# Turning the second layer's input with VectorE squares and SBUF transfers in place of TensorE transposes

## The chip, the cores and the metric

The kernel runs on one core of a Trainium2 chip. The time is the device time of one execution in microseconds; a time stated for a kernel is the median of several runs. One profiled execution gives the trace from which all durations here are read.

## The reference

Two layers (`DEPTH = 2`) of a decoder trunk over 256 tokens of width 2048, all in float32:

```python
def _layer(x, mem, positions, w_in, ...):
    (r_q, ..., z) = _split_cols(x @ w_in, IN_SPLITS)
    # four head groups: retention, latent attention, mLSTM, memory attention
    # (the last one also needs mem @ w_mem_kv)
    y = jnp.concatenate([ret, mla, mls, memo], axis=-1) * jax.nn.silu(z)
    y = y @ w_out
    return _layernorm(DEEPNORM_ALPHA * x + y, ln_g, ln_b)
```

The output of the first layer is the input `x` of the second. It is produced with tokens on the partitions, and the second layer's product `x @ w_in` wants it with features on the partitions, so it has to be turned.

## The kernel before, in words

**The stream.** Every large product is a stream of 304 slots for each layer (`SLOTS`), one slot for a tile of 128 rows of weights. Slots 0 to 15 are `memv` and 16 to 31 are `memk` (the memory's values and keys: they need `mem` alone, not `x`); slot 32 is the first of `lx0`, the first product that needs the layer's input. Float32 is multiplied as two float32r parts, high and low: ScalarE copies a weight tile to `hi` (L1067), VectorE subtracts to get `lo` (L1418), TensorE does `hi` with both parts of the input (L1331, L1332; L1346 in the layout "feat") and `lo` with the high part (L1335; L1352). `raw` has room for four pairs of slots (`RAW = 4`), `hi` and `lo` for five slots (`RING = 5`), so ScalarE and VectorE run at most five slots ahead of TensorE. SyncE (SP) loads `raw` by pairs: pair m holds slots 2m and 2m+1, and its load is issued only when `lo` of slot 2m-7 is done (L678).

**The order.** All other work is hung into this stream by tables that are written out by hand: `LATER_ACT`, `LATER_DVE` and `LATER_PE` say for the second layer after which slot of its own queue an engine does which step. Each engine, and SP too, works strictly in its own order, so a step that waits holds all that is behind it in its queue.

**The turn before.** After the first layer's normalisation ScalarE writes the normalised X in eight blocks of 128x512 (`normalise`, L845, from slot 8 to slot 18), each with its own count on `normed`. TensorE turns it in eight steps `xT` (L1115), two after each of slots 18, 22, 26 and 30, four 128x128 transposes in each, into a PSUM bank. ScalarE takes the high part from there with the gain and offset of the norm applied (`x_hi`, L863, after slots 23, 24, 27, 28, 31, 32, 35 and 36), VectorE the low part (`x_lo`, L1470 and L1477: two 128x256 scale-and-add operations to `tmp`, one subtraction). TensorE waits at slots 32, 34, 36 and 38 for `x_lo` 1, 3, 5 and 7 (L1324).

**The kernel's other turns** are made in another way: VectorE turns 32x32 squares within a block, the squares go out to DRAM (`TURN_OUT_AT`, L741) and come back in four transfers of 32 partitions each (`TURN_IN_AT`, L755, tile `turn`), which put each square in its place.

The buffer Y holds the first layer's input, later the gated product of the first layer, and from pair 22 of the second layer on its small weights (`wukv`, `wuq`, L714 and L716).

Of the kernel before, what the change touches and what calls it, by code (L numbers as in the profile page):

```python
# [130 lines left out]
def _put(table, slot, *step):  # L131
    table.setdefault(slot, []).append(step)


for _j in range(8):
    _put(LATER_PE, 18 + _j // 2 * 4, "xT", _j)
for _h in range(HEADS):
    _put(PE_AT, (71, 75, 81, 87)[_h], "mem_scores", _h)
    _put(PE_AT, 156, "mla_scores", _h)
# [14 lines left out]

ACT_AT = {}
for _j in range(8):
    _put(LATER_ACT, 8 + 3 * _j // 2, "normalise", _j)
    _put(LATER_ACT, 23 + _j // 2 * 4 + _j % 2, "x_hi", _j)
    _put(FIRST_ACT, 15 + 2 * _j, "x_hi", _j)
    if _j:  # L160
        _put(FIRST_ACT, 2 * _j - 1, "m_hi", _j + 1)
# [24 lines left out]


DVE_AT = {}
for _j in range(8):
    _put(LATER_DVE, (24, 26, 28, 30, 32, 34, 37, 38)[_j], "x_lo", _j)  # L190
    _put(FIRST_DVE, 16 + 2 * _j, "x_lo", _j)
    _put(FIRST_DVE, 22 + 2 * _j, "angles", _j)
    if _j > 2:
        _put(FIRST_DVE, 2 * _j - 1, "m_lo", _j + 1)
    _put(DVE_AT, (49, 50, 51, 52, 55, 57, 59, 60)[_j], "conv", _j)
    _put(LATER_DVE, 248 + _j, "gain", _j)
    _put(LATER_DVE, 256 + 2 * _j, "offset", _j)
# [8 lines left out]
for _s, *_step in [  # L206
# [109 lines left out]
def build_trunk(nc, a, out):  # L316
    ctx = ExitStack()
    with ctx:
# [3 lines left out]
        def signal(name, per_layer, before=0, step=1):  # L322
            return Signal(ctx.enter_context(nc.semaphore(name)), per_layer, before, step)
# [23 lines left out]
        def both(i, size):  # L347
            with nc.sbuf_tensor(f"B{i}r", [P, 4 * SEQ], F32R) as same_place:
                pass
            return sb(f"B{i}", [P, size]), same_place  # L350

        row_of = {i: both(i, 4 * SEQ) for i in (1, 2, 4, 5, 6, 7, 8, 9)}
        row_of[0] = both(0, NT * HEADS * (HD + 1))
        cols, stats = sb("cols", [P, NCOLS]), sb("stats", [P, 8, 6])
        row_of[3] = both(3, 4 * (SEQ + PAD))
# [22 lines left out]


        gb0 = gb0_place[:, :].rearrange("p (a n) -> p a n", a=2)  # L380
        xT0 = Y[:, :].rearrange("p (j w) -> p j w", j=8)
        memT = [B[i][:, 0:4 * SEQ] for i in range(4)]
        turn1 = B[4][:, 0:NT * (FR + FM)].rearrange("p (i f) -> p i f", i=NT)
# [70 lines left out]


        early = [Br[i][:, :].rearrange("p (a k t) -> p a k t", a=2, k=2) for i in (1, 2, 3, 0)]

        def y_part(part, j):

# [75 lines left out]
        first_rows = signal("first_rows", 0)  # L535
        finished, gained, diag_done = signal("finished", 0), signal("gained", 0), signal("diag_done", 0)
        scaled, copied = signal("scaled", 0), signal("copied", 0)
        first_gain = signal("first_gain", 0)
        stored = signal("stored", 0, step=16)
        dve_own, act_own = signal("dve_own", 0), signal("act_own", 0)  # L540

# [132 lines left out]
        def _(sp):  # L674
            for l in range(DEPTH):
                for m in range(PAIRS):
# [30 lines left out]
                          .then_inc(lw_in.sem, 16)  # L707
                    if m == 22:

                        if l == 0:  # L710
                            sp.wait_ge(x_lo.sem, x_lo.at(0, 7))
                        else:
                            sp.wait_ge(y_lo.sem, y_lo.at(l - 1, 7))
                        sp.dma_start(Y[:, 0:1024], a["wukv"][l:l + 1, :].rearrange("o (p n) -> p (o n)", p=P))\  # L714
                          .then_inc(mlaw_in.sem, 16)
                        sp.dma_start(Y[:, 1024:3328], a["wuq"][l:l + 1, :].rearrange("o (p n) -> p (o n)", p=P))\  # L716
                          .then_inc(mlaw_in.sem, 16)
# [15 lines left out]
                    if m == 57:  # L733
                        sp.wait_ge(mrow_out.sem, mrow_out.at(l, 0))
                        wait_job(sp, l, ("ml_q", 1))
                        sp.dma_start(B[3][:, 0:1024], a["mrow"].rearrange("h t -> (h t)").partition_broadcast(P))\
                          .then_inc(mrow_in.sem, 16)
                    if m in TURN_OUT_AT:
                        name = TURN_OUT_AT[m]
                        sp.wait_ge(squared[name].sem, squared[name].at(l, squared[name].per_layer - 1))  # L740
                        sp.dma_start(a["turn"][TURNS.index(name), :, 0:TURN_COLS[name]], squares[name]).then_inc(turn_out[name].sem, 16)  # L741
# [75 lines left out]
        def _(act):  # L817
# [20 lines left out]
            for l in range(DEPTH):  # L838
# [15 lines left out]
                def x_hi_(j):  # L854
                    if l == 0:
                        act.wait_ge(xT_in[j // 2].sem, 16)
                        act.activation(xh[:, 2 * j:2 * j + 2, :], xT0[:, j, :].rearrange("p (k t) -> p k t", k=2),
                                       ACT.Copy).then_inc(x_hi.sem, 1)
                        return
                    wait_job(act, l, ("xT", j))  # L860
                    act.wait_ge(cols_in.sem, cols_in.at(l, 0))
                    for k in (2 * j, 2 * j + 1):
                        m = act.activation(xh[:, k, :], bank(l, ("xT", j))[:, (k % 2) * 256:(k % 2 + 1) * 256], ACT.Identity,  # L863
                                           scale=cols[:, C_LNG + k:C_LNG + k + 1], bias=cols[:, C_LNB + k:C_LNB + k + 1])
                    m.then_inc(x_hi.sem, 1)

# [221 lines left out]
        def _(pe):  # L1088
# [5 lines left out]
            for l in range(DEPTH):  # L1094
                def take(*job):

                    b, u = bank_of(l, job)
                    stand_alone(pe)
                    pe.wait_ge(bank_read[b].sem, bank_read[b].at(0, u - 1))
                    return work[:, b, :]  # L1100

                def turn(dst, src):
                    return pe.transpose(dst, src, ident[0:src.shape[0], 0:src.shape[0]])  # L1103
# [8 lines left out]
                def both(parts, at):  # L1112
                    return tuple(at(x) for x in parts)

                def xT(j):  # L1115
                    pe.wait_ge(ident_in.sem, 16)
                    pe.wait_ge(normed.sem, 2 * (j // 2) + 2)
                    o = take("xT", j)
                    for kk in range(2):
                        for i in range(NT):  # L1120
                            m = turn(o[:, kk * 256 + i * P:kk * 256 + (i + 1) * P],
                                     X[:, i, (2 * j + kk) * P:(2 * j + kk + 1) * P])
                    m.then_inc(job_done.sem, 1)

                def mem_scores(h):
                    if h == 0:
                        pe.wait_ge(kq_split.sem, kq_split.at(l, 3))
# [135 lines left out]
                def ret_out(q):  # L1263
# [3 lines left out]
                    for h in (2 * q, 2 * q + 1):  # L1267
# [3 lines left out]
                        m = pe.matmul(o[:, c + P:c + 256], pt[:, 2 * P:3 * P], rv[:, 1, v], start=False, stop=True)  # L1271
                    m.then_inc(job_done.sem, 1)

                steps = {"xT": xT, "mem_scores": mem_scores, "mem_out": mem_out,
                         "ml_fold": ml_fold, "ml_q": ml_q, "gateT": gateT,
                         "ml_scores": ml_scores, "ml_out": ml_out, "mla_qr": mla_qr, "mla_kn": mla_kn,
                         "mla_qn": mla_qn, "mla_v": mla_v,
# [114 lines left out]
        def _(dve):  # L1392
# [47 lines left out]
            for l in range(DEPTH):  # L1440
# [23 lines left out]
                def x_lo_(j):  # L1464
                    dve.wait_ge(x_hi.sem, x_hi.at(l, j))
                    src, part = xT0[:, j, :].rearrange("p (k t) -> p k t", k=2), xh[:, 2 * j:2 * j + 2, :].bitcast(F32)
                    if l:
                        dve.wait_ge(cols_in.sem, cols_in.at(l, 0))
                        for k in (2 * j, 2 * j + 1):
                            m = dve.tensor_scalar(tmp[:, (k % 2) * 256:(k % 2 + 1) * 256],  # L1470
                                                  bank(l, ("xT", j))[:, (k % 2) * 256:(k % 2 + 1) * 256],
                                                  cols[:, C_LNG + k:C_LNG + k + 1], cols[:, C_LNB + k:C_LNB + k + 1],
                                                  ALU.mult, ALU.add)
                        m.then_inc(free_bank(l, "xT", j), 1)
                        wait_read(dve, l, ("xT", j))
                        src = tmp[:, :].rearrange("p (k t) -> p k t", k=2)
                    dve.tensor_tensor(xl[:, 2 * j:2 * j + 2, :], src, part, ALU.subtract).then_inc(x_lo.sem, 1)  # L1477
                    if l:
                        dve.wait_ge(x_lo.sem, x_lo.at(l, j))

                def gain(b):
                    cb, i = divmod(b, 2)
                    blk = X[:, i, cb * 512:(cb + 1) * 512]
                    if b == 0:
                        dve.wait_ge(gb0_in.sem, 16)
                        wait_job(dve, l, ("xT", 7))
                    link(dve.tensor_tensor(blk, blk, gb0[:, 0, cb * 512:(cb + 1) * 512], ALU.mult))

                def offset(b):
# [384 lines left out]
                def residual(c, *only):  # L1874
# [8 lines left out]
                    for i in only or range(NT):  # L1883
# [4 lines left out]
                steps = {"angles": angles_, "lo": lo_of, "x_lo": x_lo_, "m_lo": m_lo, "gain": gain, "offset": offset, "kept_lo": kept_lo_, "y_lo": y_lo_, "memv": memv, "mem_max": mem_max, "mem_norm": mem_norm,  # L1888
                         "mem_out": out_pair("mem_out", memo), "conv": conv, "rms": rms_, "ckv": ckv, "cqn": cqn_,
                         "kpe_rope": kpe_rope, "gates": gates, "gate_scan": gate_scan, "skip": skip, "ones": ones,  # L1890
                         "turn": turn, "turn_head": turn_head, "turn_rotary": turn_rotary, "cT": cT_, "gate_squares": gate_squares_, "ml_gap": ml_gap, "ml_weigh": ml_weigh, "ml_out": ml_out,
# [158 lines left out]
```

## Time and profile before

| | |
|---|---|
| time, median of 3 runs | 892.41 us (891.58 to 893.32) |
| time of the profiled execution | 892.57 us |
| its span | 890.8 us |
| granted TensorE clock | 0.999 |
| PE busy | 883.6 us, 99% of the span |
| VectorE busy | 661.1 us, 74% |
| ScalarE busy | 487.2 us, 55% |

The span runs from the first to the last instruction of the profile; some 1.8 us of the execution's time lie around it. "Busy" is the time in which an engine had an instruction in work. The second layer's stream begins at about 440.6 us of the span.

### The profile page before, as it was taken

How to read it: one execution, taken by the hardware profiler on the slowest of the kernel's cores; microseconds unless marked ns; L12 is line 12 of the kernel's file. 1: busy time of each engine (PE TensorE's matmuls, PEld its weight loads, DVE VectorE, ACT ScalarE, POOL GpSimd, SP SyncE). 2: the span in 40 equal slices, each digit the busy share in tenths (PEclk: the TensorE clock that was granted, in tenths of full speed). 3: DMA queues.
4: the chain of work that ended last, by engine and by line, in shares of the span. 5: the costliest groups of instructions: out<-in, count | busy, mean ns of one | idle time of the engine just before them, and what ended most of it. 6: DMA issues, size and time to landing. Idle time of an engine off the chain costs nothing.

```text
span 890.8 us, 13199 instructions
## 1 busy us (share of the span) xinstructions
PE 883.6 (99%) x4540; PEld 758.6 (85%) x4540; DVE 661.1 (74%) x1314; ACT 487.2 (55%) x914; POOL 17.4 (2%) x18
## 2 busy tenths in 40 slices
PE   9999999999999999999999999999999999999997
PEld 7888998888888888888888889888888888887896
DVE  6869697878595677766668887868677748679865
ACT  6655785545455346544476556746355553564541
POOL 0000000000000000000000000000000001000001
PEclk9999999999999999999999999999999999999999
DMA  9796587547679687665675966885484875976932
GB/s 357 281 337 200 147 268 254 177 135 229 209 219 320 210 261 247 201 190 189 191 200 185 306 229 180 258 260 169 140 280 143 292 217 165 258 220 224 356 103 95
DMA packets 70802, 198.21 MB, mean 223 GB/s; under 512 B 9288, under 2 KB 22864, under 8 KB 70096
## 3 DMA queue, kind: packets, MB, share of 16 engines
q1 hardware_dynamic: 70160, 196.33, 68.2%
q10 hardware_dynamic: 576, 1.05, 0.4%
q8 instruction: 36, 0.59, 0.3%
q14 instruction: 30, 0.25, 0.1%
HBM read 182.38 MB, written 14.95 MB: 222 GB/s over the span
## 4 chain that ended last, share of the span: by engine, by line
PE 97%; issue 1%; DVE 1%; DMA 0%; ACT 0%; POOL 0%; POOLq 0%; ACTq 0%; DVEq 0%
PE acc L1331 24%; PE acc L1332 24%; PE acc L1335 24%; PE acc L1346 10%; PE acc L1352 5%; PE work L1110 1%; PE work L1109 1%; PE work L1108 1%; PE work L1237 1%; PE work L1236 1%; PE work L1103 0%; DMA B<-in_mem_t 0%; PE work L1259 0%; PE work L1248 0%; PE work L1176 0%
## 5 line engine op out<-in xcount | busy, mean ns | idle before, releaser
L1418 DVE TENSOR_TENSOR lo<-raw,hi 128x512 fp32r<-128x512 f32 (+2 forms) x607 | 387.4, 656 | 181.4 <-ACT hi L1067 167.6
L1067 ACT ACTIVATE hi<-raw 128x512 fp32r<-128x512 f32 (+2 forms) x607 | 355.4, 603 | 297.5 <-PE acc L1335 229.2
L1331 PE MATMUL acc<-hi,xx 128*128 128x512 f32 (+2 forms) x768 | 285.4, 374 | 0.9 <-DVE xx L1514 0.9
L1332 PE MATMUL acc<-hi,xx 128*128 128x512 f32 (+2 forms) x768 | 283.5, 372 | 0.0
L1335 PE MATMUL acc<-lo,xx 128*128 128x512 f32 (+2 forms) x768 | 223.0, 372 | 0.0
L1331 PEld LDWEIGHTS acc<-hi,xx 128*128 128x128 f32 x768 | 144.6, 188 | 24.9 <-DVE xx L1514 1.3
L1332 PEld LDWEIGHTS acc<-hi,xx 128*128 128x128 f32 x768 | 144.6, 188 | 23.5
L1335 PEld LDWEIGHTS acc<-lo,xx 128*128 128x128 f32 x768 | 140.4, 188 | 24.6
L1346 PE MATMUL acc<-xx,hi 128*128 128x512 f32 x384 | 96.1, 392 | 0.0
L1346 PEld LDWEIGHTS acc<-xx,hi 128*128 128x128 f32 x384 | 69.3, 189 | 12.6
L1352 PEld LDWEIGHTS acc<-xx,lo 128*128 128x128 f32 x384 | 52.4, 190 | 3.7
L1352 PE MATMUL acc<-xx,lo 128*128 128x256 f32 x384 | 53.5, 282 | 0.0
L1331 PE MATMUL acc<-hi,mm 128*128 128x512 f32 x126 | 49.5, 392 | 0.0
L1332 PE MATMUL acc<-hi,mm 128*128 128x512 f32 x126 | 49.1, 389 | 0.0
L1335 PE MATMUL acc<-lo,mm 128*128 128x512 f32 x126 | 38.8, 389 | 0.0
L1335 PEld LDWEIGHTS acc<-lo,mm 128*128 128x128 f32 x126 | 23.7, 188 | 5.0
L1331 PEld LDWEIGHTS acc<-hi,mm 128*128 128x128 f32 x126 | 23.7, 188 | 4.9 <-issue 0.2
L1332 PEld LDWEIGHTS acc<-hi,mm 128*128 128x128 f32 x126 | 23.7, 188 | 4.7
L793 POOL TENSOR_TENSOR rstd<-stats,half 128x4 f32<-128x4 f32 (+1 forms) x6 | 9.6, 1594 | 351.0 <-DVE stats L1838 221.6
L970 ACT ACTIVATE B<-work 128x512 f32<-128x512 f32 x12 | 7.2, 596 | 14.7 <-PE work L1110 14.7
L1822 DVE TENSOR_TENSOR probT<-work,const 128x384 f32<-128x384 f32 x8 | 4.4, 554 | 13.4 <-PE work L1260 13.4
L935 ACT ACTIVATE prob<-prob,nmax 128x128 f32<-128x128 f32 (+1 forms) x16 | 7.2, 448 | 10.4 <-DVE nmax L1808 10.4
(346 smaller groups left out, 975.0 us busy)
## 6 DMA issues: line engine op xcount, KB each, us to landing
raw<-in_w SPq DMA_DIRECT2D x263, 512.0 KB, 4.4
B<-turn SPq DMA_DIRECT2D x80, 128.0 KB, 5.0
raw<-in_w SPq DMA_DIRECT2D x26, 256.0 KB, 2.7
turn<-B SPq DMA_DIRECT2D x12, 512.0 KB, 5.8
raw<-in_w SPq DMA_DIRECT2D x16, 328.0 KB, 3.3
turn<-Y SPq DMA_DIRECT2D x8, 512.0 KB, 5.5
Y<-in_wuq SPq DMA_DIRECT2D x2, 1152.0 KB, 8.8
Y<-in_x_t SPq DMA_DIRECT2D x4, 512.0 KB, 8.7
```

What stands on the lines that cost most here:

```text
L793: return pool.tensor_tensor(dst, src, half[:, 0:n], ALU.pow)
L1067: act.activation(place(l, t, hi), raw[:, s, (t % 2) * w:(t % 2 + 1) * w], ACT.Copy)\
L1108: pe.matmul(o, ah, bh, start=start, stop=False)
L1109: pe.matmul(o, al, bh, start=False, stop=False)
L1110: return pe.matmul(o, ah, bl, start=False, stop=stop)
L1236: pe.matmul(o[:, c0:c1], qnT[:, h, q], knT[:, h, 0:c1 - c0], start=True, stop=False)
L1331: pe.matmul(o, ah[:, q], hi[:, s, 0:w], start=k == 0, stop=False, skip_group_check=name == "memv")
L1332: pe.matmul(o, al[:, q], hi[:, s, 0:w], start=False, stop=False, skip_group_check=name == "memv")
L1335: m = pe.matmul(acc[:, p, i, 0:w], ah[:, i * P:(i + 1) * P], lo[:, s, 0:w], start=False, stop=k == KT - 1, skip_group_check=name == "memv")
L1346: pe.matmul(acc[:, p, j, :], hi[:, (l * SLOTS + t + u) % RING, q], x, start=k + u == 0 and kk == 0, stop=False, skip_group_check=True)
L1352: m = pe.matmul(acc[:, p, j, 0:SEQ], lo[:, s, q], both_parts[:, 2 * k + kk, 0, :], start=False, stop=2 * k + kk == KT - 1, skip_group_chec ...
L1418: dve.tensor_tensor(place(l, t, lo), raw[:, s, (t % 2) * w:(t % 2 + 1) * w], place(l, t, hi).bitcast(F32), ALU.subtract).then_inc(lo_done. ...
```

## The change

TensorE's step `xT` is gone. In its place:

- VectorE does four steps `square_x` after slots 10, 12, 13 and 15: in each, two operations that turn the 32x32 squares of a normalised 128x512 block of X. They write to `x_squares`, 16 KB a partition, in the place of the buffers B4 to B7.
- SP issues sixteen transfers from SBUF to SBUF, four after the weight load of each of the pairs 11, 12, 13 and 14. One moves 32 partitions by four runs of 1 KB, 128 KB in all, from `x_squares` to Y. Ahead of the first SP waits for all four `square_x`.
- ScalarE's `normalise` is at slots 8 to 13. Its `x_hi` are at slots 22 to 29, one a slot, and wait for all sixteen transfers; they read Y in SBUF, in runs of 32 elements, and not a PSUM bank.
- VectorE's `x_lo` are at slots 23, 25, 27, 28, 30, 32, 33 and 35 and read Y.
- `gain` no longer waits for TensorE's last `xT`.

```diff
-for _j in range(8):
-    _put(LATER_PE, 18 + _j // 2 * 4, "xT", _j)
...
-    _put(LATER_ACT, 8 + 3 * _j // 2, "normalise", _j)
-    _put(LATER_ACT, 23 + _j // 2 * 4 + _j % 2, "x_hi", _j)
+    _put(LATER_ACT, 8 + 3 * _j // 4, "normalise", _j)
+    _put(LATER_ACT, 22 + _j, "x_hi", _j)
...
+for _cb in range(4):
+    _put(LATER_DVE, (10, 12, 13, 15)[_cb], "square_x", _cb)
 for _j in range(8):
-    _put(LATER_DVE, (24, 26, 28, 30, 32, 34, 37, 38)[_j], "x_lo", _j)
+    _put(LATER_DVE, (23, 25, 27, 28, 30, 32, 33, 35)[_j], "x_lo", _j)
...
+X_IN_AT = (11, 12, 13, 14)
...
+                    if l and m in X_IN_AT:
+                        if m == X_IN_AT[0]:
+                            sp.wait_ge(x_squared.sem, 4)
+                            sp.wait_ge(y_lo.sem, y_lo.at(l - 1, 7))
+                        q = m - X_IN_AT[0]
+                        for b in range(4):
+                            sp.dma_start(Y[b * 32:(b + 1) * 32, :].rearrange("c (j a n) -> c j a n", j=4, a=4)[:, :, q],
+                                         x_squares[q * 32:(q + 1) * 32, :, b * 256:(b + 1) * 256]).then_inc(xT_in[0].sem, 16)
...
-                    wait_job(act, l, ("xT", j))
+                    act.wait_ge(xT_in[0].sem, 16 + 16 * 16)
...
+                        m = act.activation(xh[:, k, :].rearrange("p (i a r) -> p i a r", i=NT, a=4), x_block(j, k % 2), ACT.Identity,
...
+                def square_x(cb):
+                    dve.wait_ge(normed.sem, 2 * cb + 2)
+                    to = x_squares[:, cb, :].rearrange("p (b i j r) -> p i j b r", b=4, i=NT, j=4)
+                    for i in range(NT):
+                        m = dve.transpose(to[:, i], X[:, i, cb * 512:(cb + 1) * 512].rearrange("p (j b c) -> p j b c", j=4, b=4))
+                    m.then_inc(x_squared.sem, 1)
```

## Rows read from the trace of the kernel before

**Rows 1.** The page: busy time by engine, and the chain that ended last.

```profile
PE 883.6 (99%) x4540; PEld 758.6 (85%) x4540; DVE 661.1 (74%) x1314; ACT 487.2 (55%) x914; POOL 17.4 (2%) x18
PE 97%; issue 1%; DVE 1%; DMA 0%; ACT 0%; POOL 0%; POOLq 0%; ACTq 0%; DVEq 0%
```

**Rows 2.** Timeline, TensorE, slots 16 to 33 (start us, us, engine line op).

```profile
463.06 0.62 PE L1335 MATMUL acc<-lo,mm 128*128 128x512 f32 x2
...
465.78 0.62 PE L1335 MATMUL acc<-lo,mm 128*128 128x512 f32 x2
...
468.03 0.61 PE L1335 MATMUL acc<-lo,mm 128*128 128x512 f32 x2
...
487.53 2.00 PE L1346 MATMUL acc<-xx,hi 128*128 128x512 f32 x8
489.37 1.12 PE L1352 MATMUL acc<-xx,lo 128*128 128x256 f32 x8
490.32 2.00 PE L1346 MATMUL acc<-xx,hi 128*128 128x512 f32 x8
```

**Rows 3.** Chain in order of time, 464 to 490 us: start us, us, what.

```profile
466.40 0.87 PE work L1103 x8
...
485.44 0.88 PE work L1103 x8
```

**Rows 4.** Timeline, ScalarE: slot 8, first `normalise`, slot 22.

```profile
446.09 0.63 ACT L1067 ACTIVATE hi<-raw 128x512 fp32r<-128x512 f32 x1 [0.79 <-PE acc L1335]
446.63 0.80 ACT L845 ACTIVATE X<-X,ln_shift,ln_rstd 128x512 f32<-128x512 f32 x1
...
465.13 0.63 ACT L1067 ACTIVATE hi<-raw 128x512 fp32r<-128x512 f32 x1 [0.79 <-PE acc L1335]
```

**Rows 5.** Timeline, VectorE: `lo` of slot 15, and the first `x_lo`.

```profile
456.22 0.69 DVE L1418 TENSOR_TENSOR lo<-raw,hi 128x512 fp32r<-128x512 f32 x1 [0.61 <-ACT hi L1067]
...
470.02 0.99 DVE L1470 TENSOR_SCALAR tmp<-work,cols 128x256 f32<-128x256 f32 x2
...
471.77 1.30 DVE L1418 TENSOR_TENSOR lo<-raw,hi 128x512 fp32r<-128x512 f32 x2
```

**Rows 6.** VectorE, groups by form (count, busy us, mean ns of one, idle before).

```profile
L1470 DVE TENSOR_SCALAR tmp<-work,cols 128x256 f32<-128x256 f32 x16 | 7.9, 537 | 0.0
...
L1635 DVE STREAM_TRANSPOSE B<-B 128x1024 f32<-128x1024 f32 x4 | 5.0, 1239 | 0.0
...
L1759 DVE TENSOR_SCALAR B<-B,mv,rstd 128x128 f32<-128x128 f32 x16 | 4.4, 342 | 0.0
...
L1582 DVE TENSOR_SCALAR B<-B,cols 128x256 f32<-128x256 f32 x8 | 2.8, 350 | 0.1
```

**Rows 7.** Timeline, ScalarE: a pair that reads turned blocks in SBUF.

```profile
340.16 0.89 ACT L877 ACTIVATE B3r<-B,cols 128x256 fp32r<-128x256 f32 x2
```

**Rows 8.** Timeline, SP's queue: the load of `wuq`, the four transfers of one turn.

```profile
492.27 0.43 SPq L716 DMA_DIRECT2D Y<-in_wuq  x1
...
503.45 1.75 SPq L755 DMA_DIRECT2D B<-turn  x4
```

**Rows 9.** Transfers of the page: count, KB each, median us from issue to landing.

```profile
raw<-in_w SPq DMA_DIRECT2D x263, 512.0 KB, 4.4
B<-turn SPq DMA_DIRECT2D x80, 128.0 KB, 5.0
...
Y<-in_wuq SPq DMA_DIRECT2D x2, 1152.0 KB, 8.8
...
gcol<-tmp SPq DMA_DIRECT2D x8, 2.0 KB, 2.2
```

**Rows 10.** Windows of 1 us: length, granted clock, DMA share, GB/s.

```profile
503.00:504.00 1.00, 1.00 1.01 414
...
507.00:508.00 1.00, 1.00 1.09 222
```

**Rows 11.** The same in a later turn, issued from 665.98 us on.

```profile
669.00:670.00 1.00, 1.00 0.76 173
```

More of the change, by code:

```diff
@@ L350, in both, with both_x @@
             return sb(f"B{i}", [P, size]), same_place
-        row_of = {i: both(i, 4 * SEQ) for i in (1, 2, 4, 5, 6, 7, 8, 9)}
+        turned_place = {}
+        def both_x(i, size):
+            if i == 4:
+                with nc.sbuf_tensor("x_squares", [P, 4, 4 * SEQ], F32) as x_place:
+                    turned_place["x"] = x_place
+            return both(i, size)
+        row_of = {i: both_x(i, 4 * SEQ) for i in (1, 2, 4, 5, 6, 7, 8, 9)}
         row_of[0] = both(0, NT * HEADS * (HD + 1))
@@ L380, in build_trunk @@
         gb0 = gb0_place[:, :].rearrange("p (a n) -> p a n", a=2)
+        x_squares = turned_place["x"]
         xT0 = Y[:, :].rearrange("p (j w) -> p j w", j=8)
@@ L456, in build_trunk, with x_block @@
         early = [Br[i][:, :].rearrange("p (a k t) -> p a k t", a=2, k=2) for i in (1, 2, 3, 0)]
+        def x_block(j, n):
+            return Y[:, j // 2 * 1024:(j // 2 + 1) * 1024]\
+                .rearrange("p (a i j r) -> p j i a r", a=4, i=NT, j=4)[:, j % 2 * 2 + n]
         def y_part(part, j):
@@ L537, in build_trunk @@
         scaled, copied = signal("scaled", 0), signal("copied", 0)
-        first_gain = signal("first_gain", 0)
+        first_gain, x_squared = signal("first_gain", 0), signal("x_squared", 0)
         stored = signal("stored", 0, step=16)
@@ L708, in _ @@
                     if m == 22:
[L710 to L713, printed above, removed]
+                        sp.wait_ge(x_lo.sem, x_lo.at(l, 7))
                         sp.dma_start(Y[:, 0:1024], a["wukv"][l:l + 1, :].rearrange("o (p n) -> p (o n)", p=P))\
@@ L859, in x_hi_ @@
                         return
-                    wait_job(act, l, ("xT", j))
+                    act.wait_ge(xT_in[0].sem, 16 + 16 * 16)
                     act.wait_ge(cols_in.sem, cols_in.at(l, 0))
                     for k in (2 * j, 2 * j + 1):
-                        m = act.activation(xh[:, k, :], bank(l, ("xT", j))[:, (k % 2) * 256:(k % 2 + 1) * 256], ACT.Identity,
+                        m = act.activation(xh[:, k, :].rearrange("p (i a r) -> p i a r", i=NT, a=4), x_block(j, k % 2), ACT.Identity,
                                            scale=cols[:, C_LNG + k:C_LNG + k + 1], bias=cols[:, C_LNB + k:C_LNB + k + 1])
@@ L1113, in both @@
                     return tuple(at(x) for x in parts)
[L1115 to L1123, printed above, removed]
                 def mem_scores(h):
@@ L1272, in ret_out @@
                     m.then_inc(job_done.sem, 1)
-                steps = {"xT": xT, "mem_scores": mem_scores, "mem_out": mem_out,
+                steps = {"mem_scores": mem_scores, "mem_out": mem_out,
                          "ml_fold": ml_fold, "ml_q": ml_q, "gateT": gateT,
@@ L1469, in x_lo_ @@
                         for k in (2 * j, 2 * j + 1):
-                            m = dve.tensor_scalar(tmp[:, (k % 2) * 256:(k % 2 + 1) * 256],
-                                                  bank(l, ("xT", j))[:, (k % 2) * 256:(k % 2 + 1) * 256],
+                            m = dve.tensor_scalar(tmp[:, (k % 2) * 256:(k % 2 + 1) * 256].rearrange("p (i a r) -> p i a r", i=NT, a=4),
+                                                  x_block(j, k % 2),
                                                   cols[:, C_LNG + k:C_LNG + k + 1], cols[:, C_LNB + k:C_LNB + k + 1],
                                                   ALU.mult, ALU.add)
-                        m.then_inc(free_bank(l, "xT", j), 1)
-                        wait_read(dve, l, ("xT", j))
+                        link(m)
                         src = tmp[:, :].rearrange("p (k t) -> p k t", k=2)
@@ L1485, in gain @@
                         dve.wait_ge(gb0_in.sem, 16)
-                        wait_job(dve, l, ("xT", 7))
                     link(dve.tensor_tensor(blk, blk, gb0[:, 0, cb * 512:(cb + 1) * 512], ALU.mult))
@@ L1886, in residual @@
                     return m
-                steps = {"angles": angles_, "lo": lo_of, "x_lo": x_lo_, "m_lo": m_lo, "gain": gain, "offset": offset, "kept_lo": kept_lo_, "y_lo": y_lo_, "memv": memv, "mem_max": mem_max, "mem_norm": mem_norm,
+                steps = {"angles": angles_, "lo": lo_of, "x_lo": x_lo_, "m_lo": m_lo, "square_x": square_x, "gain": gain, "offset": offset, "kept_lo": kept_lo_, "y_lo": y_lo_, "memv": memv, "mem_max": mem_max, "mem_norm": mem_norm,
                          "mem_out": out_pair("mem_out", memo), "conv": conv, "rms": rms_, "ckv": ckv, "cqn": cqn_,
```

## The prediction

> **What bounds the kernel now.** I read the page first. It shows TensorE busy for 99% of the span and holding 97% of the chain that ended last [rows 1], so the reader is to see that a microsecond off TensorE's queue is a microsecond off the time, and that every wait put on it costs in full. Next the chain in order of time around the turn: the transposes are on it, in four pieces of eight [rows 3]. Then each engine's timeline, to see how far ScalarE and VectorE run ahead, and last SP's queue, the landing times and the DMA windows, since the change moves the turn there.
>
> **A clock of slots.** Two slots of the memory products take 465.78 - 463.06 = 2.72 us on TensorE, 1.36 each; the slot with transposes behind it takes 468.03 - 465.78 = 2.25 [rows 2]. Without any transpose slot 19 would begin 0.45 us after 465.78, at 466.23, and so slot 23 at 466.23 + 4 x 1.36 = 471.67. The pair of slots 32 and 33 begins at 487.53 and a pair takes 2.79 us [rows 2]; without the four groups it would begin near 484.0, and the pair 36 and 37 at 489.6.
>
> **Removed.** Four pieces of 0.87 or 0.88 us [rows 3]: 3.5 us off TensorE, all on the path. This is the whole gain; nothing else on TensorE changes.
>
> **Added ahead of the transfers.** ScalarE now does eight `normalise` in slots 8 to 13. From 446.09, with 0.54 us for a `hi` and 0.80 for a block [rows 4], that ends at 446.1 + 6 x 0.54 + 8 x 0.80 = 455.7. TensorE does not reach slot 13 until 458, so this is hidden by the lead of four to five slots. The squares are not shown at 128x512; 1024 columns take 1.24 us [rows 6], so one lies between 0.62 (half) and 0.69 (a 128x512 subtraction [rows 5]). I take 0.65, eight of them 5.2 us. They hold up `lo` of slots 11 to 15: `lo` 10 is done near 450.7, then five `lo` at 0.61 and the squares: 450.7 + 3.1 + 5.2 = 459.0, against 456.9 before [rows 5]. TensorE wants `lo` 16 at 463, so this too costs nothing. But the transfers begin only then: SP passes its wait at about 459.5.
>
> **The transfers.** SP needs 1.75 us for four issues [rows 8], so 7.0 for sixteen and some 1.2 for the three weight loads between them: the last is issued at 467.7 at the earliest. Landing time is the unknown. From below: the only SBUF-to-SBUF transfers of the trace, of 2 KB, land after 2.2 us [rows 9], which gives 469.9; with the 5.0 us of the 128 KB transfers of a turn [rows 9] it is 472.7. By bytes: sixteen times 128 KB is 2.1 MB, and the weight loads of pairs 11 to 14 are another 2.1 MB in the same engines. The weight loads move at 414 GB/s when the engines are full [rows 10], 1.27 us each, 5.1 in all. The turns' transfers, of the same shape (32 partitions, runs of 1 KB) but from DRAM, pull the rate down to 222 and 173 GB/s [rows 10, 11], in windows in which weights still take a part. I take 200 GB/s for them: 10.5 us. Sum 15.6 from 459.5: 475.1, and with the first transfer's latency T = 475.5 for the landing of the last. With 173 GB/s and a microsecond more it is 477.7. The range of T is 469.9 to 477.7.
>
> The Trainium skill says in "SBUF — State Buffer", section "Door 1: The DMA port swizzle", that a transfer on 32 partitions reaches only half of SBUF's ports, measured there at 189 GB/s for 1 MiB. The rows agree as far as they go (173 and 222 GB/s where the turns run); by its figure 2.1 MB would take an estimated 11.1 us in place of 10.5, and the sum would rise by 0.6.
>
> **Who waits.** `x_hi` 0 stands behind slot 22 in ScalarE's queue and waits for all sixteen. ScalarE starts `hi` 22 at 465.13 [rows 4], so it is there by 465.8 and stands until T; behind it in its queue is `hi` 23, for which VectorE's `lo` 23 and TensorE's slot 23 wait. An `x_hi` pair from SBUF costs 0.8 [rows 7], then `hi` 0.63: `hi` 23 is there at T + 1.4. TensorE wants it at 471.67. By this alone TensorE loses T - 470.2: at 475.5, 5.3 us. Before, the same step hung behind a transpose of slot 18, and ScalarE never stood.
>
> VectorE stands as well, and has all eight `x_lo` left. One took 1.75 us (470.02 to 471.77 [rows 5]). Reading SBUF, its two scale-and-add operations cost between 0.35 each (one column operand [rows 6]) and 0.54 as before; with two column operands 128 columns already take 0.34 [rows 6], so I take 0.41, and 1.5 for an `x_lo` (1.4 to 1.75). From T + 1.4 to the end of `lo` 37 it has fifteen `lo` at 0.61, eight `x_lo` and the `memk` turn of 1.24: 9.2 + 12.0 + 1.24 = 22.5, so T + 23.9. TensorE wants `lo` 37 at 489.6 + 2.3 = 491.9 (the `lo` part of a pair starts 1.84 into it, 487.53 to 489.37 [rows 2], its second half 0.5 later). Loss: T - 468.0; with the bounds of `x_lo`, T - 468.9 to T - 466.1. This is the larger one and decides: at 475.5 it is 7.5 us. After slot 38 VectorE's `lo` alone is less than TensorE's slot, and the lead comes back; `raw` is not late, for the pairs up to 14 have long been loaded.
>
> **Sum.** -3.5 + 7.5 = +4.0 us on the profiled execution's 892.57 us (span 890.8, 1.8 around it), 896.6; that execution lies 0.16 above the median, so I say 896.5. Bounds: T 469.9 with the cheapest `x_lo` gives -3.5 + 1.0 = -2.5, 890.1; T 477.7 with the dearest gives -3.5 + 11.6 = +8.1, 900.7. The gain is eaten from T = 471.5 on.
>
> **Rivals.**
>
> *The transfers are quick and the gain stays.* The place is ScalarE's wait at slot 22. If a transfer within SBUF has no DRAM in its way, only SP's issue holds it, and T is 469.9: with the cheapest `x_lo` 890.1, and if ScalarE's and VectorE's lead covers all of it, 892.57 - 3.5 = 889.1. It decides below T = 471.5, and shows by over 0.2% below 469.7. For it speak the 2.2 us of the small ones; against it SP's last issue at 467.7 and the rates of the turns. The Trainium skill ("DMA: Bandwidth & Descriptors", section "Why small descriptors are slow (HBM only)") says that transfers within SBUF do not pay for small descriptors; by its 435 GB/s for the fabric the bytes would need an estimated 4.8 us, and no run here shows it. Chance 0.10.
>
> *A draw.* The transfers move nearly like weights: T between 469.7 and 473.3, landing 5 us after the last issue. The loss on TensorE then equals the gain within 1.8 us: at T = 472.7 it is 4.7 - 3.5 = +1.2, 893.8, and about 892.5 in the middle. The change does what it says, and the time does not move. Chance 0.20.
>
> *The lateness is passed on.* SP issues the second layer's `wuq` at pair 22, when `lo` 37 is done; it takes 8.8 us to land [rows 9], and ScalarE needs it at slot 45. Before, TensorE reached slot 46 (seven pairs of 2.79 after 487.53 [rows 2], 507.1) 15 us after the issue at 492.3 [rows 8]; after, with `lo` 37 only just in time, about 11. With 8.8 + 0.83 + 0.63 for the first of its steps 0.5 us is left, and a transfer that is 2 us slower costs 1.5. With the high bounds: 898.5 to 901. Chance 0.15.
>
> **How the numbers follow.** Forecast as above (T 473.3 to 477.7, loss 5.3 to 9.7 us, 894.4 to 898.8): 0.55; quick 0.10; draw 0.20; passed on 0.15. A measurement of this kernel tells some 0.2%, 1.8 us, from no change. Faster by more than that: the quick case, 0.10. Within it: the draw, 0.20. Slower: 0.70. The range leaves out the quick end below 891.0 and the far end of the last case above 900.7: some 0.09 and 0.06, and the rest is in the width of T.
>
> **What the profile after would show.** No L1103 on TensorE between slots 18 and 30 and slots of 1.36 us up to slot 22 (the 3.5 us). A wait of ScalarE on the DMA of Y of some 9 to 10 us behind `hi` 22 (T at 475.5); under 5 us would be the quick case. TensorE idle 4 to 6 us at slot 23, with ScalarE's `hi` as the releaser, then small waits on `lo` up to slot 37, 7 to 8 us together. DMA windows near 200 to 270 GB/s at full share between 460 and 475. Squares of 0.62 to 0.69 us; `x_lo` of 1.4 to 1.6. What would make me wrong above all: a rate of the SBUF transfers over 300 GB/s, or a start of the transfers well ahead of 459.5.

## The result, and the profile after

| | before | after |
|---|---|---|
| time, median | 891.78 us (891.58 to 893.32) | 901.57 us (900.13 to 901.90) |
| profiled execution | 892.57 us | 900.13 us |
| its span | 890.8 us | 898.3 us |
| granted TensorE clock | 0.999 | 0.996 |
| PE busy | 883.6 us | 882.1 us |

The kernel became slower by 1.04%: the ratio is 1.0104, 95% interval 1.0093 to 1.0114. Both columns have five runs of one session, and the rows below come from the profiled executions. These differ by 7.5 us and the medians by 9.8; after's profiled execution is the shortest of its five (1.4 us under their median), before's lies 0.8 above its own.

The page of after, its first busy row and the shares of the chain, against [rows 1]:

```profile
PE 882.1 (98%) x4508; PEld 756.4 (84%) x4508; DVE 662.6 (74%) x1322; ACT 486.6 (54%) x914; POOL 17.8 (2%) x18
PE 91%; DVE 2%; DMA 2%; issue 2%; ACT 1%; SPq 1%; POOL 0%; POOLq 0%; ACTq 0%; DVEq 0%
```

TensorE has 32 instructions fewer, the transposes, but its share of the chain that ended last fell from 97 to 91%: the end now hangs on other engines for part of the time. The waits of 440 to 520 us say where (engine, line, waited for: us in total, times, longest):

```profile
ACT xx L883 <- DMA Y<-x_squares: 11.7, 1, 11.7
...
PE acc L1341 <- ACT hi L1087: 7.3, 1, 7.3
ACT mm L930 <- DMA Y<-in_wuq: 2.7, 1, 2.7
ACT hi L1087 <- DMA raw<-in_w: 2.2, 2, 1.5
...
PE acc L1362 <- DVE lo L1428: 1.0, 1, 1.0
PE acc L1356 <- ACT hi L1087: 0.9, 1, 0.9
...
PE acc L1345 <- DVE lo L1428: 0.3, 1, 0.3
```

The rows that begin with PE add up to 9.5 us; before, TensorE was busy for every one of these 80 us. The wait of the first row (ScalarE, for the transfers) is the cause of the 7.3 us of TensorE. ScalarE's timeline, against [rows 4]:

```profile
465.16 0.63 ACT L1087 ACTIVATE hi<-raw 128x512 fp32r<-128x512 f32 x1 [0.79 <-PE acc L1345]
477.51 1.09 ACT L883 ACTIVATE xx<-Y,cols 128x256 fp32r<-128x256 f32 x2 [11.72 <-DMA Y<-x_squares]
478.51 0.61 ACT L1087 ACTIVATE hi<-raw 128x512 fp32r<-128x512 f32 x1
479.03 1.08 ACT L883 ACTIVATE xx<-Y,cols 128x256 fp32r<-128x256 f32 x2
```

`hi` of slot 22 (465.16) begins within 0.03 us of where it began before. Then ScalarE stands for 11.72 us in `x_hi` 0, until 477.51, which is T, the landing of the last transfer. `hi` 23 follows it. TensorE's timeline, against [rows 2]; the rows with a bracket are its waits:

```profile
471.25 0.61 PE L1345 MATMUL acc<-lo,mm 128*128 128x512 f32 x2
479.17 0.79 PE L1341 MATMUL acc<-hi,mm 128*128 128x512 f32 x1 [7.31 <-ACT hi L1087]
...
481.90 0.46 PE L1341 MATMUL acc<-hi,mm 128*128 128x512 f32 x1
...
490.12 0.74 PE L1345 MATMUL acc<-lo,mm 128*128 128x512 f32 x2 [0.26 <-DVE lo L1428]
...
493.46 1.98 PE L1356 MATMUL acc<-xx,hi 128*128 128x512 f32 x8
...
502.48 0.71 PE L1362 MATMUL acc<-xx,lo 128*128 128x256 f32 x4 [0.98 <-DVE lo L1428]
503.03 2.00 PE L1356 MATMUL acc<-xx,hi 128*128 128x512 f32 x8
...
515.23 2.08 PE L1356 MATMUL acc<-xx,hi 128*128 128x512 f32 x8 [0.87 <-ACT hi L1087]
```

Read against an even pace of 1.36 us a slot and 2.79 a pair, this is an account of all that was lost: slot 23 begins at 479.17 in place of 471.70 (+7.5); slot 23 takes 481.90 - 479.17 = 2.73 us (+1.4); slots 24 to 31 take 11.56 in place of 10.9 (+0.7); the `lo` products of slot 37 wait for VectorE (503.03 - 493.46 less three pairs, +1.2); slot 46 waits for `hi`, behind `wuq` and a late `raw` (515.23 - 503.03 less four pairs, +1.0). That is 11.8 lost and 3.5 gained, +8.3, of which 7.5 are left at the end of the span.

VectorE and the queue of SP, against [rows 5] and [rows 8]:

```profile
457.89 1.30 DVE L1494 STREAM_TRANSPOSE x_squares<-X 128x512 f32<-128x512 f32 x2
...
479.76 0.73 DVE L1480 TENSOR_SCALAR tmp<-Y,cols 128x256 f32<-128x256 f32 x2
480.53 0.69 DVE L1486 TENSOR_TENSOR xx<-tmp,xx 128x512 fp32r<-128x512 f32 x1
481.26 0.69 DVE L1428 TENSOR_TENSOR lo<-raw,hi 128x512 fp32r<-128x512 f32 x1
```

```profile
459.22 2.55 SPq L756 DMA_DIRECT2D Y<-x_squares  x4
461.81 0.60 SPq L700 DMA_DIRECT2D raw<-in_w  x1
...
469.34 2.54 SPq L756 DMA_DIRECT2D Y<-x_squares  x4
```

Two squares take 1.30 us in the row and the next `lo` begins 1.22 after them; an `x_lo` takes 481.26 - 479.76 = 1.50. The first issue is at 459.22, but four take 2.55 us, not 1.75, and the sixteenth issue, begun at 471.27, ends at 471.9. That transfer lands 6.22 us after its issue began:

```profile
471.27 6.22 DMA Y<-x_squares
...
502.73 0.43 SPq L726
...
503.68 9.49 DMA raw<-in_w
```

These are pieces of the chain in order of time. L726 issues `wukv`; `wuq` follows at 503.21, 10.9 us later than before. The last row is the load of pair 23 (slots 46 and 47), issued directly behind the two. It lands after 9.49 us, at 513.2, and ScalarE, which has waited 2.7 us for `wuq`, waits another 0.71 for it ahead of `hi` of slot 46. So a late `raw` has a part in the 1.0 us lost at slot 46. The windows (length, busy time of the engines, granted clock, DMA share, GB/s), against [rows 10, 11]; rows without the busy times are from a view that leaves them out:

```profile
459.00:463.00 4.00, 4.00 (x19) 3.33 (x18) 2.75 (x5) 1.83 (x3) 0.00 (x0) 1.00 0.80 233
463.00:467.00 4.00, 4.00 (x20) 3.30 (x19) 3.76 (x6) 1.33 (x3) 0.00 (x0) 1.00 1.05 276
467.00:471.00 4.00, 4.00 (x19) 3.32 (x18) 0.80 (x2) 0.00 (x0) 0.00 (x0) 1.00 1.03 243
471.00:475.00 4.00, 0.86 (x4) 0.38 (x2) 0.00 (x0) 0.00 (x0) 0.00 (x0) 1.00 1.08 248
475.00:476.00 1.00, 0.59 0.75 135
476.00:477.00 1.00, 0.50 0.21 67
...
480.00:482.00 2.00, 2.00 (x6) 1.51 (x6) 1.88 (x4) 2.00 (x5) 0.00 (x0) 0.50 0.48 121
482.00:484.00 2.00, 2.00 (x10) 1.65 (x9) 1.81 (x4) 2.00 (x5) 0.00 (x0) 1.00 0.42 162
```

The DMA engines are full from 463 to 475 and move 243 to 276 GB/s in those windows: that is what the transfers and the weights get together. After 476 they are nearly idle, though the last transfer is seen to land only at 477.5. The granted clock falls in the window from 475 to 476 (0.59) and is 0.50 (1.2 GHz) from 476 to 482, after TensorE had stood since 471.9, and 1.00 again from 482 on; hence the slot of 2.73 us.

### The profile page after: what moved, and what is told of

Read it like the earlier page. It is cut to its first block, busy times and chain, and to the rows that moved or that the text cites. A ratio compares the mean times of both kernels' runs of the same rounds, so it can differ in the third digit from the quotient of the medians.

```text
span 898.3 us, 13151 instructions
## 1 busy us (share of the span) xinstructions
PE 882.1 (98%) x4508; PEld 756.4 (84%) x4508; DVE 662.6 (74%) x1322; ACT 486.6 (54%) x914; POOL 17.8 (2%) x18
## 4 chain that ended last, share of the span: by engine, by line
PE 91%; DVE 2%; DMA 2%; issue 2%; ACT 1%; SPq 1%; POOL 0%; POOLq 0%; ACTq 0%; DVEq 0%
PE acc L1342 23%; PE acc L1341 23%; PE acc L1345 23%; PE acc L1356 8%; PE acc L1362 4%; PE work L1130 1%; PE work L1129 1%; PE work L1128 1%; DMA raw<-in_w 1%; DVE lo L1428 1%; DMA Y<-x_squares 1%; PE work L1246 1%; PE work L1247 1%; ACT hi L1087 1%; SPq L756 0%
## 5 line engine op out<-in xcount | busy, mean ns | idle before, releaser
L1345 PEld LDWEIGHTS acc<-lo,mm 128*128 128x128 f32 x126 | 23.9, 190 | 5.6 <-DVE lo L1428 0.7
L883 ACT ACTIVATE xx<-Y,cols 128x256 fp32r<-128x256 f32 x16 | 8.7, 591 | 11.7 <-DMA Y<-x_squares 11.7
L1837 DVE TENSOR_TENSOR probT<-work,const 128x384 f32<-128x384 f32 x8 | 4.4, 554 | 12.6 <-PE work L1270 12.6
```

The costliest lines, as they stand in the source:

```text
L1345: m = pe.matmul(acc[:, p, i, 0:w], ah[:, i * P:(i + 1) * P], lo[:, s, 0:w], start=False, stop=k == KT - 1, skip_group_check=name == "memv")
```

## The experiments

Ten kernels ran, in three groups, each group beside runs of the kernel before on its own chip (medians 891.51, 891.52 and 891.41 us). Unless it is said otherwise, an edit is made to the kernel after, and a ratio is to the kernel before, with its 95% interval.

### The gain alone, and the traffic alone

```diff
-X_IN_AT = (11, 12, 13, 14)
+X_IN_AT = ()
...
-                    act.wait_ge(xT_in[0].sem, 16 + 16 * 16)
```

This leaves out the transfers. `x_hi` and `x_lo` read the normalised X where it lies, so the second layer works on an input that isn't turned; squares and all other steps stay.

> The kernel after without the sixteen transfers; x_hi and x_lo read unturned X in SBUF in the same shape, so the second layer computes with an unturned input. Theory (the gain is the 3.5 us of transposes and all the rest of the result is the wait): 891.8 - 3.5 = 888.3 us, no idle of TensorE at slot 23, granted clock full. Rival (the squares on VectorE or the SBUF reads cost the path something by themselves): 890 us or more.

Measured: 888.70 us (887.90 to 891.52), ratio 0.9970 [0.9960, 0.9979]. So the transposes on TensorE were worth 2.8 us by the medians and 3.4 by the shortest executions (887.90 against before's 891.32), where 3.5 had been put down. TensorE has no wait from 440 to 520 us in this run; squares, the earlier `normalise` and the steps that read SBUF cost little or nothing.

The second kernel issues all sixteen transfers, but still nobody on ScalarE or VectorE waits for them or reads what they bring; the input is again not turned. SP alone waits, before the buffers of the squares and Y are written again:

```diff
                     if m == 20:
+                        if l:
+                            sp.wait_ge(xT_in[0].sem, 16 + 16 * 16)
...
-                    act.wait_ge(xT_in[0].sem, 16 + 16 * 16)
```

> As the run without transfers, but all sixteen transfers are issued as in the kernel after and nobody on ScalarE or VectorE waits for them (SP waits for them before it loads over their source and destination). The input of the second layer is again unturned. Theory (only the wait of ScalarE costs): within 1 us of the run without transfers, 888 to 889.5. Rival (4.2 MB in 16 us hold up the weight loads themselves): ScalarE waits for raw at slots 24 to 30 and the time is 892 or more.

Measured: 891.50 us (889.24 to 893.17), ratio 0.9992 [0.9981, 1.0004], between the two expected results and nearer to the rival. The two intervals do not meet: the traffic by itself takes back 2.8 us, the whole gain, with no wait placed on it. ScalarE's timeline shows how; while the transfers run the load of `raw` is late three times, 2.3 us in all, where there was no such wait before or without the transfers:

```profile
469.14 0.63 ACT L1089 ACTIVATE hi<-raw 128x512 fp32r<-128x512 f32 x1 [0.52 <-DMA raw<-in_w]
...
473.32 0.63 ACT L1089 ACTIVATE hi<-raw 128x512 fp32r<-128x512 f32 x1 [1.05 <-DMA raw<-in_w]
...
477.20 0.63 ACT L1089 ACTIVATE hi<-raw 128x512 fp32r<-128x512 f32 x1 [0.76 <-DMA raw<-in_w]
```

In its windows the DMA engines are at 1.01 to 1.08 of their time from 464 to 476 with 267 to 279 GB/s, against 0.39 to 0.60 before. ScalarE waits for `raw` for 5.9 us in all from 440 to 520 (3.7 without the transfers, all of it after 501 us; none before), and TensorE stands twice:

```profile
493.53 0.71 PE L1364 MATMUL acc<-xx,lo 128*128 128x256 f32 x4 [1.03 <-DVE lo L1430]
...
506.45 1.84 PE L1358 MATMUL acc<-xx,hi 128*128 128x512 f32 x7 [1.06 <-ACT hi L1089]
```

The first is `lo` of slot 37, which without the transfers is in time; the second is slot 46, behind `wuq` and the load of pair 23, for which ScalarE waits 2.1 and 1.46 us here, 1.2 and 1.37 without the transfers.

### Fewer bytes, and a second queue

```diff
-                        for b in range(4):
+                        for b in ((0, 1) if q % 2 == 0 else (2, 3)):
...
-                    act.wait_ge(xT_in[0].sem, 16 + 16 * 16)
+                    act.wait_ge(xT_in[0].sem, 16 + 8 * 16)
```

Eight transfers in place of sixteen; the other half of Y isn't written, and is read as it lies.

> Only eight of the sixteen transfers are sent and waited for (half of Y keeps old values). With 200 GB/s for these bytes the last lands 5.2 us earlier, near 471 to 472, ScalarE's wait is 6 us, TensorE's idle at slot 23 about 1.5 us, the clock does not fall: 893 to 895 us. If a fixed latency and not the amount sets the landing, it stays above 475 and the time above 898.

Measured: 896.86 us (896.53 to 898.25), ratio 1.0057 [1.0042, 1.0072], 2 us above what was expected. T comes 3.7 us earlier, at 473.8: 0.46 us for each 128 KB left out, 283 GB/s at the margin. Eight issues of SP are gone with them, so this run alone doesn't tell bytes from issues; the next one does. The time falls by 4.7. Half of the bytes don't take away half of the 18.3 us from the first issue to T, for weights and latency stay.

```diff
-                        for b in range(4):
+                        for b in range(2):
...
+                    pool.wait_ge(x_squared.sem, 4)
+                    for q in range(4):
+                        for b in (2, 3):
+                            pool.dma_start(Y[b * 32:(b + 1) * 32, :]..., x_squares[...]).then_inc(x_pool.sem, 16)
...
```

The same sixteen transfers, eight of them issued by GpSimd, with ScalarE waiting for both counts.

> Half of each four transfers is issued by GpSimd, which is idle, all eight of them at once when the squares are done, with a count of its own. If SP's issue (0.64 us each, 10.3 us in all) sets the landing, the last transfer lands some 4 to 5 us earlier, near 473, and the time falls to about 896. If the bytes in the DMA engines set it, the landing stays at 476 to 478 and the time at 900 to 902.

Measured: 901.28 us (901.13 to 901.53), ratio 1.0103 [1.0088, 1.0118], the time of the kernel after. Its row of issues:

```profile
459.66 4.52 POOL L822 DMA_DIRECT2D Y<-x_squares x8 [13.75 <-DVE x_squares L1503]
```

All eight are out by 464.2, yet ScalarE's wait is 12.6 us (11.7 after). From issue to landing GpSimd's take 3.5 to 8.8 us. SP's own eight still stand behind weight loads, so its last issue begins at 470.0, only 1.3 us earlier than after, but that transfer lands after 8.49 us in place of 6.22. So SP's dear issues, though they are on the chain of after, don't set T: issued earlier, the transfers lie longer in the engines, and the bytes set it.

### The shape and the order of the transfers

```diff
-                            sp.dma_start(Y[b * 32:(b + 1) * 32, :].rearrange("c (j a n) -> c j a n", j=4, a=4)[:, :, q],
-                                         x_squares[q * 32:(q + 1) * 32, :, b * 256:(b + 1) * 256]).then_inc(xT_in[0].sem, 16)
+                            sp.dma_start(Y[:, q * 1024 + b * 256:q * 1024 + (b + 1) * 256],
+                                         x_squares[:, q, b * 256:(b + 1) * 256]).then_inc(xT_in[0].sem, 16)
```

Sixteen transfers of the same 128 KB in runs of 1 KB, but over all 128 partitions; the squares don't get to their places.

> The sixteen transfers have the same bytes, the same runs of 1 KB and the same places in SP's queue, but each copies 256 columns of all 128 partitions to the same partitions of Y (so Y gets the squares unplaced, and the input is wrong). If the shape of 32 partitions makes the transfers slow, the last lands near 473 (limited by SP's last issue at 471.9), ScalarE's wait falls from 11.7 to 7 or 8 us and the time to about 896 to 897. If the bytes and the runs of 1 KB within SBUF are slow in any shape, the landing stays at 476 to 478 and the time at 900 to 902.

Measured: 898.47 us (897.45 to 899.38), ratio 1.0077 [1.0064, 1.0091], between the two expected results. ScalarE's wait is 9.86 us, so T comes 1.9 us earlier in its queue, and the time is 3.1 us less. Its windows of 459 to 475 are at 0.75 to 0.91 of the engines' time with 257 to 271 GB/s, the same bytes for less of it. The shape has a part in T, at least 1.9 us of it. How much more is not shown: here the engines are no longer full, SP's last issue begins at 471.30 and its transfer lands 4.61 us later, so SP's issues may hold T in this run. Wide transfers from two queues were not tried. The Trainium skill's rule that a transfer on 32 partitions reaches only half of SBUF's ports ("SBUF — State Buffer", section "Door 1: The DMA port swizzle") points the same way; by its 189 GB/s the forecast T would have been an estimated 476.1, still short of 477.5.

```diff
-                        for b in range(4):
+                        for b in (0, 2, 1, 3):
```

> The kernel after with the four transfers of each group in the order of target partitions 0, 64, 32, 96 (from 0, 32, 64, 96), so that neighbours in the queue write different halves of the partitions. If neighbours in the queue hold each other up because they write the same half, the landing is 2 us or more earlier and the time 898 to 899.5. If not, the landing stays at 477 to 478 and the time at 901 to 902.

Measured: 900.70 us (899.47 to 902.22), ratio 1.0098 [1.0083, 1.0114], and a wait of 12.3 us on ScalarE: no difference that can be told. In its trace one issue of SP took 2.35 us and the last began at 473.3, so T says little here; the time decides.

### The clock

```diff
+for _j in range(4):
+    _put(LATER_PE, 22, "fill", _j)
...
+                def fill(j):
+                    o = take("fill", j)
+                    for n in range(7):
+                        m = pe.matmul(o, mm[:, 0, 0, 0:P], mm[:, 0, :, :].rearrange("p a t -> p (a t)"), start=True, stop=True)
...
```

28 products that nobody uses stand behind slot 22, so that TensorE works through the wait.

> 28 products of 128x512 that nobody reads stand on TensorE behind slot 22, 6.3 us of work in the 7.9 us in which it was idle; nothing else changes. If the low clock after the idle stretch costs the two slow slots (2.73 against 1.36 us), the granted clock stays full and the time falls by 1.4 us, to about 900.2. If the low clock is only seen in the idle stretch and costs nothing, the time stays at 901.6.

Measured: 901.02 us (899.92 to 903.66), ratio 1.0106 [1.0089, 1.0123]. TensorE's timeline:

```profile
471.76 6.51 PE L1140 MATMUL work<-mm 128*128 128x512 f32 x28
479.83 0.50 PE L1350 MATMUL acc<-hi,mm 128*128 128x512 f32 x1 [1.56 <-ACT hi L1089]
...
481.34 0.50 PE L1350 MATMUL acc<-hi,mm 128*128 128x512 f32 x1
```

The windows up to 484 show a granted clock of 1.00, and slot 23 takes 481.34 - 479.83 = 1.51 us in place of 2.73. The time is the same. Slot 23 starts 0.66 us later than after (T was later too), and the wait for the last `lo`, at 503.15, is again 0.67 later: nothing of the faster slot is left there. From T on it is VectorE that sets slot 37, and ScalarE's pair of `x_hi` and `hi` takes 1.50 us (478.51 and 480.01) against TensorE's 1.36. The half clock was real, but it was hidden.

### The wait at another place

```diff
-    _put(LATER_ACT, 22 + _j, "x_hi", _j)
+    _put(LATER_ACT, (31, 31, 32, 33, 34, 35, 36, 37)[_j], "x_hi", _j)
...
-    _put(LATER_DVE, (23, 25, 27, 28, 30, 32, 33, 35)[_j], "x_lo", _j)
+    _put(LATER_DVE, (31, 31, 33, 33, 35, 35, 37, 37)[_j], "x_lo", _j)
```

The `memk` turn of VectorE goes to slot 38, out of the way. The computation is whole.

> The same sixteen transfers at the same places, but x_hi stands behind slots 31 to 37 (from 22 to 29), x_lo behind 31 to 37 and the memk turn behind 38. Theory (the wait stands too early in ScalarE's queue): x_hi 0 comes just as the last transfer lands, TensorE does not idle at slot 23, and only VectorE's eight x_lo before slot 38 cost 1 to 3 us: 889.5 to 891.5. Rival (eight x_lo, eight x_hi and fifteen slots cannot be done between 477.5 and slot 38): a loss of 5 us or more there, 894 or more.

Measured: 896.03 us (893.87 to 897.55), ratio 1.0042 [1.0025, 1.0058]: 5.5 us less than after, and still slower than before. The hole at slot 23 is gone, but two other costs come up, in ScalarE's and in TensorE's timeline:

```profile
473.34 1.16 ACT L1089 ACTIVATE hi<-raw 128x512 fp32r<-128x512 f32 x2 [3.14 <-DMA raw<-in_w]
477.25 1.15 ACT L1089 ACTIVATE hi<-raw 128x512 fp32r<-128x512 f32 x2 [2.75 <-DMA raw<-in_w]
480.41 1.16 ACT L1089 ACTIVATE hi<-raw 128x512 fp32r<-128x512 f32 x2 [2.01 <-DMA raw<-in_w]
```

```profile
485.71 2.06 PE L1358 MATMUL acc<-xx,hi 128*128 128x512 f32 x8 [1.22 <-ACT hi L1089]
489.81 2.11 PE L1358 MATMUL acc<-xx,hi 128*128 128x512 f32 x8 [1.10 <-DVE xx L1488]
494.01 2.11 PE L1358 MATMUL acc<-xx,hi 128*128 128x512 f32 x8 [1.14 <-DVE xx L1488]
498.21 2.12 PE L1358 MATMUL acc<-xx,hi 128*128 128x512 f32 x8 [1.14 <-DVE xx L1488]
```

ScalarE and VectorE reach slots 32 to 38 with little lead, since `raw` was late, and have two `x_lo` of 1.5 us in each pair of slots beside its two `lo`: 4.2 us a pair (489.81 to 494.01), where TensorE needs 2.79. Four waits, 4.6 us, are the remaining loss.

### Half by transfers, half by TensorE

TensorE turns the blocks of `x_hi` 0 to 3 as the kernel before did, behind slots 18 and 22; the sixteen transfers carry only the other half, 64 KB each.

```diff
+for _j in range(4):
+    _put(LATER_PE, 18 + _j // 2 * 4, "xT", _j)
...
-    _put(LATER_ACT, 22 + _j, "x_hi", _j)
+    _put(LATER_ACT, (23, 24, 27, 28, 30, 31, 32, 33)[_j], "x_hi", _j)
...
-for _cb in range(4):
+for _cb in (2, 3):
...
-    _put(LATER_DVE, (23, 25, 27, 28, 30, 32, 33, 35)[_j], "x_lo", _j)
+    _put(LATER_DVE, (24, 26, 28, 30, 32, 33, 35, 36)[_j], "x_lo", _j)
```

> TensorE turns the first half of the features (four of its eight steps, 1.75 us), the squares and transfers the second half, with sixteen transfers of 64 KB, and x_hi 4 to 7 wait for them behind slots 30 to 33. The last transfer lands near 475, x_hi 4 is reached near 478, so nobody waits: half the gain, 891.8 - 1.7 = 890.1. If transfers of half the size are no quicker and late again, TensorE idles at slot 31 and the time is above 893.

Measured: 891.00 us (890.22 to 892.47), ratio 0.9993 [0.9984, 1.0001]. Nobody waits for the transfers, each lands after 2.1 to 3.8 us, and this is TensorE's only wait from 440 to 520 us:

```profile
506.62 2.08 PE L1376 MATMUL acc<-xx,hi 128*128 128x512 f32 x8 [0.42 <-ACT hi L1097]
```

It is the fastest kernel here that computes the whole, and it can't be told from the kernel before: half of 3.5 us is 1.75, and the trace shows part of it going to the same two places, `raw` (ScalarE waits 2.3 us) and `wuq` (2.5 us).

To take `wuq` out, its steps were moved two slots back:

```diff
-    _put(ACT_AT, 45 + _k, "wuq", _k)
-    _put(DVE_AT, 46 + _k, "lo", "wuq", _k)
+    _put(ACT_AT, 47 + _k, "wuq", _k)
+    _put(DVE_AT, 48 + _k, "lo", "wuq", _k)
```

> As the version in which TensorE turns half, and the steps that split wuq stand two slots later, so that its late landing no longer holds hi of slot 46. The 0.7 us of idle TensorE behind it should go: 890.3. If VectorE is the one that is late there (its conv steps begin at slot 49), the time stays at 891 or goes up.

Measured: 892.49 us (891.72 to 893.15), ratio 1.0009 [1.0001, 1.0018]. The wait for `wuq` is gone and a wait for `raw` of 3.7 us stands in the same stretch; TensorE waits 0.6 us for a `lo`. It gained nothing, and the issues of SP say why. The load that is late is that of pair 23 again: issued at 494.36, directly behind `wukv` and `wuq`, it lands after 9.5 us, just when `hi` of slot 46 begins (503.86). The same load takes 9.5 to 9.7 us in the kernel after, without the transfers, with them unread and in the half version; in the kernel before, where it was issued 3.9 us behind `wuq`, it takes 6.0. Moving the steps of `wuq` uncovers that wait; it doesn't take it away.

## Why the prediction was right or wrong

The direction and the mechanism were right: 3.5 us are taken off TensorE, one wait of ScalarE at slot 22 holds `hi` 23, `lo` of slot 37 is late after it, and `wuq` behind that. The time was forecast at 896.5 us and measured at 901.57, beyond the upper bound of 900.7; on the profiled execution the forecast change was +4.0 and the measured one +7.5 us. Two steps of the sum failed. T, the landing of the last transfer, was sized too small: 16.0 us from the first issue, measured 18.3. And what comes behind T was put too low: the term T - 468.0 gives 9.5 us with the measured T, where 10.8 were lost up to slot 38, and slot 46, with `wuq` and `raw` late, was put at nothing and cost 1.0. By the steps:

- **"3.5 us off TensorE."** Right in kind; 2.8 by medians, 3.4 by the shortest executions, when nothing is transferred.
- **Squares, "I take 0.65".** Two in 1.22 to 1.30 us: 0.61 to 0.65. The last ended at 459.2, and SP's first issue is at 459.22 (forecast 459.5).
- **"SP needs 1.75 us for four issues."** 2.55, and the three weight loads between them take 2.2 in place of 1.2. The last issue ends at 471.9, not 467.7. It is wrong, but it costs nothing here: with half the issues on another queue T does not come earlier.
- **"With the first transfer's latency T = 475.5."** This is the term that decides, and it was too small: 477.5. From the first issue on 4.2 MB took 18.3 us, where 16 were forecast. The sum had put weights at 414 GB/s and transfers at 200, one after the other, 15.6 us, a mean of 269 GB/s; the windows of 4 us in which both run show 233 to 276. With the 256 GB/s of 463 to 475 the bytes need an estimated 16.4 us, 0.8 more. The rest lies at the ends: the engines are at 0.80 of their time from 459 to 463, and at 0.21 in the microsecond from 476, while the landing is seen at 477.5; the sum had 0.4 us for all latency. The upper bound, 477.7, held it by 0.2 us. The transfers' narrow shape accounts for at least 1.9 us of T (the wide ones), the order for nothing that the time shows, the bytes for 0.46 us a transfer.
- **"An `x_hi` pair from SBUF costs 0.8."** 0.99 (0.59 an operation); with `hi` 1.50 us. `hi` 23 is there at T + 1.6, forecast T + 1.4.
- **"TensorE loses T - 470.2."** 7.3 by the formula with the measured T, 7.3 in the row of the wait, 7.5 by the pace.
- **"I take 0.41, and 1.5 for an `x_lo`."** 406 ns and 1.50 us.
- **"Loss: T - 468.0."** 9.5 with the measured T. By the account the loss up to slot 38 is 10.8. `lo` 37 is there near 502.3, T + 24.8 in place of T + 23.9: the first `lo` begins 0.2 late, and VectorE stands 0.65 us in three waits before it, two of them for ScalarE's `hi`.
- **"`raw` is not late."** This was wrong, and it was left out of every bound. The transfers alone cost 2.8 us, with `raw` late while they run and again at slot 46; with the wait placed later ScalarE waits 12.5 us for `raw` from 440 to 520, one of the two costs there. In the kernel after itself it is hidden up to T, for ScalarE stands anyway while `raw` comes in, but not at slot 46: the 0.71 us are on TensorE's path, and without them an estimated 0.2 of its 0.87 us of waiting would be left.
- **"The lateness is passed on" (chance 0.15).** It came on top of the forecast: `wuq` was issued at 503.21, ScalarE waited 2.7 us for it and 0.7 for the `raw` issued behind it, which the prediction had not seen, and TensorE lost 1.0 at slot 46. It had been given a condition, the high bounds, and the condition was met.

The miss on the profiled execution adds up as +2.0 for T, +1.3 for the queues behind it, +1.0 for slot 46, less 0.8 that TensorE regained later: +3.5. The rest of the distance between 896.5 and 901.57 lies between the medians and the profiled executions, and the rows of one execution can't say where. The clock, which had not been foreseen, slows slot 23 but is not in this sum: keeping TensorE busy did not shorten the time.

The two quick rivals fail on T: 469.9 or 473.3 at most were needed. The Trainium skill ("DMA: Bandwidth & Descriptors", section "Why small descriptors are slow (HBM only)") counts SBUF-to-SBUF transfers as unharmed by small descriptors, and its section "Specifications" gives 435 GB/s for the fabric. The transfers and the weights together did not reach it: in windows of 4 us 276 GB/s was the most in 459 to 475 us of after, and wide ones got 271; single microseconds show up to 336 and 344.

Open stays what holds the full DMA engines at 240 to 280 GB/s: no run moved the transfers without the weight stream beside them, and the wide ones ran against SP's issues. Open, too, is why executions of one kernel spread over up to 4 us (889.24 to 893.17 in the second one). The 19 beside it of the kernel before lie within 2.1 (891.32 to 893.39), but in the next group one of its 17 was at 895.13, 3.8 above the shortest.

## What to carry to other kernels

To take work off the bound engine pays only if its replacement's last byte lands within the lead that the engines around it have. Here T had to come by 470.2, 11.0 us after the first issue, and the transfers needed 18.3; the 7.3 us between are TensorE's wait. Price the replacement's bytes as well, not its wait alone: beside a weight stream that takes 0.4 to 0.6 of the DMA time 2.1 MB cost 2.8 us with nobody waiting for them, as much as the change could bring. And where a step waits for a transfer in a queue worked strictly in order, place it behind as much of that queue as the rest allows: here later places of `x_hi` and `x_lo` were worth 5.5 us, until VectorE, with two `x_lo` a pair, became too slow. Look, too, at what is issued right behind a big load: the weights of pair 23 landed 9.5 us after their issue behind `wukv` and `wuq`, and moving the steps of `wuq` only uncovered the wait for them.

## What the runs showed of the hardware that had not been expected

- An issue of a transfer from SBUF to SBUF of 32 partitions took SP 0.59 to 0.63 us in the kernel after (single ones up to 2.35 in other runs), against 0.44 for one of the same size from DRAM [rows 8]; on GpSimd's queue 0.55.
- 128 KB transfers within SBUF landed after 3.0 to 6.2 us with the weight stream beside them (median 4.8), wide ones after 2.6 to 4.6, and 64 KB ones after 2.1 to 3.8.
- TensorE's granted clock was 0.50 from 476 to 482 us of after (0.59 in the microsecond before), after the engine had stood since 471.9; the slot in it took 2.73 us, against 1.51 after the same wait filled with products.
- The scale-and-add with two column operands takes 406 ns from SBUF where it took 537 from PSUM [rows 6]; a 128x512 turn of squares takes as long as a subtraction of that size (0.61 to 0.69 us).
